# The routed experts of a two-block transformer on one Trainium2 core: all first products before all second products, with the first results in DRAM between them

## What is computed

```python
def one_block(xblk):
    q = (xblk @ w_query).reshape(B, TOKEN_BLOCK, N_PEER_HEADS, 2, SUBKEY_DIM)
    s = jnp.einsum('bthpd,hpnd->bthpn', q, sub_keys).astype(jnp.float32)
    vals, idx = lax.top_k(s, PEER_TOPK)
    cand = (vals[..., 0, :, None] + vals[..., 1, None, :]).reshape(...)
    cand_idx = (idx[..., 0, :, None] * N_KEYS + idx[..., 1, None, :]).reshape(...)
    top_s, pos = lax.top_k(cand, PEER_TOPK)
    eidx = jnp.take_along_axis(cand_idx, pos, axis=-1)
    g = jax.nn.softmax(top_s, axis=-1).astype(xblk.dtype)
    h = jnp.einsum('btd,bthkd->bthk', xblk, expert_u[eidx])
    act = jax.nn.gelu(h, approximate=False) * g
    return jnp.einsum('bthk,bthkd->btd', act, expert_v[eidx])
```

## Time and profile before

| | us |
|---|---|
| median of 3 runs (4229.99 to 4234.79) | 4233.03 |
| the profiled execution | 4228.66 |
| its span in the trace | 4226.9 |
| TensorE busy | 3918.0 (93%) |
| VectorE, ScalarE, GpSimd busy | 2746.0, 1996.5, 96.7 |
| layer 0, from the end of the sub-key scores to the last expert product | 421.1 to 1430.1 |
| layer 1, the same | 1765.2 to 2771.9 |

### The profile page before, as it was taken

One profiled execution on the slowest core, in us unless ns is written; L12 is line 12 of the kernel. 1 busy time (PEld: TensorE's weight loads), 2 busy tenths in 40 slices (PEclk: granted clock), 3 DMA queues, 4 the chain that ended last, 5 costly groups with the idle time before them and its releaser, 6 DMA issues.

```text
span 4226.9 us, 77624 instructions
## 1 busy us (share of the span) xinstructions
PE 3918.0 (93%) x25828; PEld 3362.6 (80%) x25828; DVE 2746.0 (65%) x5370; ACT 1996.5 (47%) x3973; POOL 96.7 (2%) x96
## 2 busy tenths in 40 slices
PE   6989499999999999859999999989999989898998
PEld 2989146999999888714799999979998779898897
DVE  1563976776667665597676677756666665666665
ACT  1554065445544554327554445444454444444444
POOL 0000000000000000000000000001001010101010
PEclk6999599999999999869999999999999999999999
DMA  8435644555555434654455555565554225454453
GB/s 285 153 112 170 243 145 146 186 188 185 188 187 186 163 115 150 209 184 164 153 186 186 188 185 187 186 193 184 167 186 137 93 66 186 140 186 139 140 179 134
DMA packets 195903, 714.34 MB, mean 169 GB/s; under 512 B 21696, under 2 KB 22080, under 8 KB 195520
## 3 DMA queue, kind: packets, MB, share of 16 engines
q1 hardware_dynamic: 194112, 705.08, 50.0%
q0 software_dynamic: 1664, 7.57, 0.7%
HBM read 711.52 MB, written 1.05 MB: 169 GB/s over the span
## 4 chain that ended last, share of the span: by engine, by line
PE 84%; DVE 10%; ACT 2%; DMA 2%; issue 1%; PEldq 0%; SPq 0%; DVEq 0%; ACTq 0%; PEld 0%; POOL 0%
PE bank L1620 16%; PE bank L1622 16%; PE bank L1621 16%; PE bank L1675 8%; PE bank L1676 8%; PE bank L1677 8%; PE bank L1793 4%; PE bank L1955 2%; PE bank L1738 2%; DMA raw<-stream 2%; PE bank L1956 1%; DVE wl L954 1%; PE bank L1926 1%; PE bank L2080 1%; DVE arena L1318 0%
## 5 line engine op out<-in xcount | busy, mean ns | idle before, releaser
L954 DVE TENSOR_TENSOR wl<-raw,wh 128x512 fp32r<-128x512 f32 x2180 | 1508.0, 704 | 1032.0 <-ACT wh L529 999.1
L529 ACT ACTIVATE wh<-raw 128x512 fp32r<-128x512 f32 x2180 | 1345.6, 630 | 1214.0 <-PE bank L1622 758.4
L1620 PE MATMUL bank<-XH,wh 128*128 128x256 f32 x5184 | 1499.3, 289 | 94.3 <-DVE XL L1056 46.1
L1621 PE MATMUL bank<-XL,wh 128*128 128x256 f32 x5184 | 1483.5, 286 | 0.0
L1622 PE MATMUL bank<-XH,wl 128*128 128x256 f32 x5184 | 1483.0, 286 | 0.0
L1620 PEld LDWEIGHTS bank<-XH,wh 128*128 128x128 f32 x5184 | 1008.9, 195 | 129.3 <-issue 79.1
L1621 PEld LDWEIGHTS bank<-XL,wh 128*128 128x128 f32 x5184 | 1012.0, 195 | 14.0 <-issue 1.0
L1622 PEld LDWEIGHTS bank<-XH,wl 128*128 128x128 f32 x5184 | 1010.9, 195 | 0.0
L1675 PE MATMUL bank<-wh,AH 128*128 128x512 f32 x1464 | 574.4, 392 | 0.0
L1676 PE MATMUL bank<-wl,AH 128*128 128x512 f32 x1464 | 573.9, 392 | 0.0
L1677 PE MATMUL bank<-wh,AL 128*128 128x512 f32 x1464 | 569.6, 389 | 0.0
(11 more groups left out here) (237 smaller groups left out, 3458.5 us busy)
## 6 DMA issues: line engine op xcount, KB each, us to landing
raw<-stream SPq DMA_DIRECT2D x1340, 512.0 KB, 3.3
arena<-rpb POOLq DMA_DIRECT2D x4, 1024.0 KB, 20.5
arena<-tables POOLq DMA_DIRECT2D x2, 832.0 KB, 7.4
X<-x_t SPq DMA_DIRECT2D x1, 1024.0 KB, 7.6
arena<-ctx_t POOLq DMA_DIRECT2D x1, 1024.0 KB, 6.4
out_t<-X SPq DMA_DIRECT2D x4, 256.0 KB, 2.1
arena<-tables POOLq DMA_DIRECT2D x1, 608.0 KB, 8.8
cols<-columns SPq DMA_DIRECT2D x1, 218.0 KB, 2.5
```

Of the source, the lines that this page charges most:

```text
L529: act.activation(wh[:, n % 4, :], raw[:, q % 4, HALF * half:HALF * (half + 1)], ACT.Copy).then_inc(hi_ready, 1)
L954: tt_op(wl[:, n % 4, :], raw[:, q % 4, HALF * half:HALF * (half + 1)], wh[:, n % 4, :].bitcast(F32), SUB).then_inc(lo_ready, 1)
L1620: pe.matmul(out, wh[:, n % 4, a:b], moving_h, start=start, stop=False, skip_group_check=check)
L1621: pe.matmul(out, wh[:, n % 4, a:b], moving_l, start=False, stop=False, skip_group_check=check)
```

## The change

**Stream.** `experts.l` becomes `expert_u.l` (128 units) and `expert_v.l` (128 units), each in order. The conditioning stages (`MIXED_ADA`: `ada1.1`, `ada2.0` in layer 0, `ada2.1`, `ada2.2` in layer 1; 96 units per layer) are laid between the first 120 units of `expert_u` in the ring: nine places hold five first-product units and four conditioning units.

**Phase one,** 128 steps u, written out without a loop. TensorE: the first product of tile u, a conditioning unit (four steps of five), at times two transposes, from u = 61 a batch of gates. VectorE: the routing instructions with `feed()`, the low half of the next tile, between them; then per step a `lo` and two one-hots. ScalarE: the high halves of tile u + 1, from u = 60 the weighted one-hots, gelu of tile u into `HS` (two buffers), from u = 62 the copy of a bank into the gates. The gates' product is now of plain fp32 one-hots: four matmuls a batch. All one-hots live in a new area `side`, no longer in `wh`, `wl`. GpSimd issues the store of each gelu result (128 KB) to `h_spill` in DRAM; gelu of u + 2 waits for it.

**Phase two.** SyncE loads the stored results back (four buffers `HV`, in `side`) and the units of `expert_v`, alternately. VectorE multiplies a result by its gates (`gated`, one tile ahead), ScalarE makes the high part `AH` (before: VectorE), VectorE the low part `AL`; TensorE runs the second products alone, back to back.

```diff
-        add(f"ada2_gates.{l}", KT * ADA2_GATES, False)
-        add(f"experts.{l}", 2 * KEYS, True, KEYS)
+        for name in MIXED_ADA[l]:
+            add(name, 48, False)
+        add(f"expert_u.{l}", KEYS, True, KEYS)
+        add(f"expert_v.{l}", KEYS, True)
...
+        u = out[f"expert_u.{l}"]
+        for k in range(MIXED_U):
+            ring[base + 9 * (k // 5) + 2 * (k % 5)] = (u, k)
+        for k in range(MIXED_U, KEYS):
+            ring[base + MIXED_A + k] = (u, k)
+        for a in range(MIXED_A):
+            st = out[MIXED_ADA[l][a // 48]]
+            ring[base + 9 * (a // 4) + 2 * (a % 4) + 1] = (st, a % 48)
...
+        def load_values(l):
+
+            st = stages[f"expert_v.{l}"]
+            sp.wait_ge(onehots_free, 2 + BATCHES * (l + 1))
+            for j in range(8):
+                if j >= 4:
+                    sp.wait_ge(gate_done, KEYS * l + j - 3)
+                sp.wait_ge(h_stored[j % 2], 16 * (KEYS // 2 * l + j // 2 + 1))
+                load_h(l, j)
+                load(st.q + j)
+            for n in range(2):
+                sp.wait_ge(h_stored[n], 16 * KEYS // 2 * (l + 1))
...
-            pick_vectors(f"ada2_gates.{l}", 2)
+            U = stages[f"expert_u.{l}"]
+            for u in range(KEYS):
+                pool.wait_ge(group_free, 2 + U.g + u + 1)
+                pool.dma_start(h_spill[u, :, :], HS[:, u % 2, :]).then_inc(h_stored[u % 2], 16)
...
+                group_done(U, u)
+                if l or u >= 2:
+                    act.wait_ge(h_stored[u % 2], 16 * (KEYS // 2 * l + u // 2))
+                act.activation(HS[:, u % 2, :], banks[4 + (U.g + u) % 2][:, 0:T], ACT.Gelu).then_inc(group_free, 1)
...
+            for b in range(BATCHES):
+                feed()
+                if b or l:
+                    dve.wait_ge(weighted_ready, first + b)
+                tt_op(batch(unweighted), keys, over_tokens(0, b), ALU.is_equal).then_inc(unweighted_ready, 1)
+                dve.wait_ge(onehots_free, first + b + 1)
+                tt_op(batch(hot_j[:, b % 2, :]), keys, over_tokens(1, b), ALU.is_equal).then_inc(onehots_ready, 1)
...
+            with dve.Fori(0, KEYS // 4 - 1) as i:
+                for j in range(2, 6):
+                    lo(V, j, i, 4)
+                    row_lows(j, i)
+                    gated(j + 1, i, 4 * i)
...
+            for u in range(KEYS):
+                pe.wait_ge(group_free, U.g + u + 1)
+                tile(U, u, 0, 0, banks[4 + (U.g + u) % 2][:, 0:T], first_pair)
+                if u == 0:
+                    pe.wait_ge(route_evacuated, 8 * (l + 1))
+                for a in after(u):
+                    ada_unit(first_block + a // KT, a % KT, place[MIXED_ADA[l][a // 48], a % 48])
+                n = block_after(u, 3)
+                if n is not None:
+                    turn_block(first_block + n)
...
+                b = u - GATES_FROM - 1
+                if 0 <= b < BATCHES:
+                    spread_choices(b)
```

More of the change, by code:

```diff
@@ L113, in plan @@
     add("ffn.1.1", 3 * FF_TILES, True, FF_TILES)
-    out, q, s, r, g = {}, 0, 0, 0, 0
+    out, ring, q, s, r, g = {}, {}, 0, 0, 0, 0
     for name, units, split, source, groups in rows:
         out[name] = Stage(name, units, split, source, q, s, r, g)
+        if name.startswith("expert_u"):
+            l = int(name[-1])
+            mix(l, out[MIXED_ADA[l][0]].q)
+        elif not any(name in names for names in MIXED_ADA):
+            for k in range(units):
+                ring[q + k] = (out[name], k)
         q += units
@@ L121, in plan @@
         g += groups
-    return out, placed
+    return out, ring, placed
 COLUMNS = [("c", KT), ("c_2", KT), ("c_ctx", KT), ("final_norm", KT)]
@@ L190, in __call__, with build @@
         return self.at[name]
-def build(nc, ctx, stream, columns, tables, x_in, ctx_in, rpb, out):
-    stages, _ = plan()
+def build(nc, ctx, stream, columns, tables, x_in, ctx_in, rpb, h_spill, out):
+    stages, ring, _ = plan()
+    place = {(st.name, k): q for q, (st, k) in ring.items()}
     made = operands_made()
@@ L408, in _, with released, load @@
         seen = Seen()
-        def released(unit):
-            for st in stages.values():
-                if st.q <= unit < st.q + st.units:
-                    k = unit - st.q
-                    return (lo_ready, 2 * (st.s + k) + 2) if st.split else (raw_used, st.r + k + 1)
+        def released(q):
+            st, k = ring[q]
+            return (lo_ready, 2 * (st.s + k) + 2) if st.split else (raw_used, st.r + k + 1)
+        def load(q):
+            st, k = ring[q]
+            if q >= 4:
+                sp.wait_ge(*released(q - 4))
+            sp.dma_start(raw[:, q % 4, :], stream[st.source + k, :, :]).then_inc(raw_ready[q % 4], 16)
         sp.dma_start(cols[:, :], columns).then_inc(prepared, 16)
@@ L1783, in rows_times @@
-        def rows_times(st, nv, kt, halves=(0, 1), i=0, first=False, last=False):
-            q = st.q + kt
-            n_rows = nv * st.units // KT
-            if kt == 0 and halves[0] == 0:
-                pe.wait_ge(picked, 2 * (blocks[0] + 1) + 2 * i)
-            if halves[0] == 0:
-                pe.wait_ge(raw_ready[q % 4], 16 * (q // 4 + 1) + 32 * i)
-            for half in halves:
-                matmul = pe.matmul(banks[6 + half][0:n_rows, :], pick[:, kt, nv:nv + n_rows],
-                                   raw[:, q % 4, HALF * half:HALF * (half + 1)],
-                                   start=first and kt == 0, stop=last and kt == KT - 1)
-            if halves[-1] == 1:
-                matmul.then_inc(raw_used, 1)
@@ L1819, in _, with ada_unit @@
-        pe.wait_ge(silu_ready, 1)
-        ada("ada1.0")
-        pe.wait_ge(mod_copied, ada_stages[0])
+        def ada_unit(n, kt, q):
+            if kt == 0 and n >= 2:
+                pe.wait_ge(block_copied, n - 1)
+            pe.wait_ge(raw_ready[q % 4], 16 * (q // 4 + 1))
+            for g in range(GROUPS):
+                matmul = pe.matmul(banks[6 + n % 2][GROUP * g:GROUP * (g + 1), 0:BLOCK], vectors[:, kt, :],
+                                   raw[:, q % 4, BLOCK * g:BLOCK * (g + 1)], start=kt == 0, stop=kt == KT - 1,
+                                   tile_position=(0, GROUP * g))
+            matmul.then_inc(raw_used, 1)
@@ L1822, in _ @@
+        pe.wait_ge(silu_ready, 1)
+        for k in range(48):
+            ada_unit(k // KT, k % KT, stages["ada1.0"].q + k)
+            if k > KT and k % KT == 1:
+                turn_block(k // KT - 1)
+        turn_block(5)
+        pe.wait_ge(block_placed, 6)
         for l in range(DEPTH):
@@ L1971, in _, with spread_choices @@
-            turn(st, 2)
-            pe.wait_ge(mod_copied, ada_stages[0])
-            pairs(stages[f"experts.{l}"], 1)
+            U, V = stages[f"expert_u.{l}"], stages[f"expert_v.{l}"]
+            first, first_block = l * BATCHES, 6 + BLOCKS_PER_LAYER * l
+            def spread_choices(b):
+                pe.wait_ge(gate_banks_free, first + b + 1)
+                pe.wait_ge(onehots_ready, first + b + 1)
+                pe.wait_ge(weighted_ready, first + b + 1)
+                for n in range(BATCH):
+                    at = slice(n * P, (n + 1) * P)
+                    last = pe.matmul(banks[b % 2][:, at], by_weight[:, b % 2, at], hot_j[:, b % 2, at], start=True,
+                                     stop=True)
+                last.then_inc(onehots_free, 1)
```

491 lines of the change are left out of this document (227 added, 264 removed).

## The result

| | before | after |
|---|---|---|
| median us (lowest to highest, 4 runs each, same chip) | 4231.51 (4229.99 to 4234.79) | 3926.78 (3925.54 to 3928.62) |
| ratio, 95% interval | | 0.9279 (0.9263 to 0.9295) |
| profiled execution, its span | 4228.66, 4226.9 | 3927.0, 3925.1 |
| layer 0, sub-key scores to last second product | 1009.0 | 855.0 (423.3 to 1278.3) |
| layer 1, the same | 1006.6 | 857.4 (1611.8 to 2469.1) |

The forecast was 3944 us, in a range of 3885 to 4035. The two layers gave 2015.6 - 1712.4 = 303.2 us, and the profiled executions differ by 301.7: the gain lies in the expert layers and nowhere else.

A forecast was written before the change was run, and what follows sets the result against it. Routing was taken as bound by VectorE, gates and experts by TensorE. Per layer, TensorE's 837.4 us plus 20, 3, 2 and 1 gave 863.4, saving 288.8 over both layers: 3944 us, range 3885 to 4035.

The forecast's parts named there:

- turned blocks, choices: Phase one, TensorE: 12 turned blocks and the turned choices take about 6 us per layer.
- second products, change of phase, start: Phase two, per layer: 352.0 us of second products, 2 for the change of phase, 1 for the start.
- The ada unit: Phase one, TensorE: a conditioning unit between tiles costs 0.5 us against 0.43 in a row; 96 units, 48 us per layer.
- list of what would prove it wrong: Wrong if ScalarE waits on stores at gelu, phase two exceeds 2.8 us, or an ada unit between tiles exceeds 0.6.
- The waits in tiles 0 to 60: First 60 tiles: 18 us per five against TensorE's 16.35, so 20 us a layer, plus 3 for table loads.
- The batches: Tiles 61 to 124: a gates batch takes TensorE 1.0 us, 0.1 of it to change over; 64 us per layer.
- Second products: Phase two: TensorE takes 2.75 us per tile, 352.0 per layer, and hides all other engines' work.
- The store path: First results stored to DRAM in phase one: 5.5 us in all, fits two buffers, cost 0.
- slower by the stores: Rival, phase one: a 9.6 us store path would cancel the gain; at 12 us, 4540 us in all; chance 0.05.
- VectorE as the bound of phase two: Rival, second products: VectorE waits for ScalarE's high rows, 3.1 us a tile, 4034 us in all; chance 0.06.
- The ring: Rival, first 60 tiles: four load places set the pace, 20.7 us per five; 4009 us, 4030 with batches; chance 0.10.

## Why the prediction was right, point by point

The time was right to 17 us of 3927 (0.4%), the forecast was the case that came, and the mechanism is shown: the routing and the gates run beside first products, and taking either out brings its time back. But three terms of the sum were mis-sized, by +24, -18 and -7 us a layer, and cancelled each other. That is in part luck: only the first two hang together.

| per layer, us | predicted | measured |
|---|---|---|
| 128 first products | 367.4 | 368.6 (2.88 each) |
| 96 ada units | 48 (0.5 each) | 72 (0.75 each) |
| 64 batches | 64 (1.0 each) | 57 (0.89 each) |
| turned blocks, choices | 6 | 3 (0.2 each, choices 0.65) |
| waits in tiles 0 to 60 | 20 and 3 | 4 to 6 |
| second products, change of phase, start | 352, 2, 1 | 349 |
| sum | 863.4 | 855.0 and 857.4 |

(The measured rows add up to 1 to 2 us less than the layers.)

- **The ada unit** failed as a step: "between tiles of another shape I take 0.5". 0.43 in a row was right, and the 0.07 added for the change of shape should have been 0.32. It was on the prediction's own list of what would prove it wrong (over 0.6), and it cost 24 us a layer. What makes it so is not the shape of the matmul but the division of the array: four column groups of 32 between whole-array matmuls, as the run with the unit on the whole array showed.
- **The waits in tiles 0 to 60** failed in the other direction: 18 us per five tiles against TensorE's 16.35. TensorE's five tiles were really 3.54 + 3 x 3.63 + 2.97 = 17.4 us (3.54 for the tile that has no unit before it), so that they covered VectorE's 16.5 and the DMA engines' 16.6 by 0.8, where the prediction had them 0.2 short, and the waits almost vanished. The two errors hang together: a filler that takes longer hides more. Without the units these tiles stopped at 204 to 208 us, 16.7 to 17.0 per five, where I had put the two at 16.5 and 16.6.
- **The batches** were 0.89, just the eight records of the earlier trace rows without the 0.1 for a change: a whole-array fp32 matmul behind a whole-array fp32r matmul costs no change.
- **Second products** at 2.75 were 2.73 with no first products between them; the 0.02 may be the change of kind at the borders, which the earlier trace rows has in each.
- **The store path** was 4.2 us (0.3 handing over, 3.9 landing, in all 256 between 2.0 and 6.1) against 5.5; two places cover it, and ScalarE waits at most 5 us in all for stores. The rival "slower by the stores", from a path of 9.6 us, was far off: even with one place the kernel stays 5.1% ahead of the one before. The Trainium skill's rule that GpSimd's descriptor writing stalls while VectorE runs an instruction in a two-port mode (SBUF — State Buffer, the "DVE blocks DMA" trap) shows nothing here: the issue took 539 to 570 ns in 256 stores, with VectorE busy for 0.83 of that time in tiles 2 to 59, against the 0.54 of the earlier trace rows. Nearly all of VectorE's work there is on two tensors or the search for the top 16; plain copies, which the rule is about, are few and of 0.2 to 0.6 us, so the rule was hardly put to the test.
- **VectorE as the bound of phase two** was not near: its order has the gate of a tile ready one tile ahead, as the prediction said, and even 0.29 us more a tile cost nothing.
- **The ring** as pace setter did not come by itself, but stands close: pairs of units seem to bring it (8 to 13 us a layer, after what they save), and 12% more bytes bring the DMA engines.

The 4 to 6 us of waits in tiles 0 to 60 have two parts in the trace. In each layer TensorE waits five times for VectorE's low halves, 1.9 and 2.1 us in all, four of them at the same tiles (17, 35, 44, 55) in both layers, which speaks for VectorE's order of steps. Three times it waits for ScalarE's gelu, 1.7 and 3.6 us. The longest, in layer 1, on ScalarE and then TensorE:

```profile
1626.55 1.15 ACT L565 ACTIVATE wh<-raw 128x512 fp32r<-128x512 f32 x2 [4.04 <-DMA raw<-stream]
1627.61 0.36 ACT L819 ACTIVATE side<-bank 128x256 f32<-128x256 f32 x1
1628.05 0.36 PE L1705 MATMUL bank<-XH,wh 128*128 128x256 f32 x1 [1.76 <-ACT side L819]
```

Gelu stands behind the high halves of the next tile, and those waited for a load that landed 7.1 us after its issue, the slowest of these tiles, where the median is 4.6. What stays open is why single loads are so late; taking the stores' bytes away left the waits about as they were (1.1 and 3.6 us in layer 0), and more than four places were not tried.

## What to carry to other kernels

Price a filler between two instructions of another kind from a place where it stands between them, not in a row of its own; where it divides the array in column groups and its neighbours don't, add the change (0.32 us here) once for each time that it is entered, and put fillers in groups where the ring of loads has slack. When one engine's term in a sum grows, take the waits that it covers down again: the terms aren't independent. A result that goes out to DRAM and back in bulk cost nothing here while the places before it covered one landing and the DMA engines had room (0.88 busy; with each store doubled, 0.92, it cost 13.5 us a layer), and how many places are needed is (gelu + hand-over + landing) over the time of a tile: 4.6 / 3.6 gives two.

## What the runs showed of the hardware

- Changing TensorE from the whole array to 32-column groups and back costs 0.32 us at full clock; four matmuls in four such groups take the time of one.
- An fp32 matmul of 128 columns costs 0.22 us and may stand between fp32r matmuls at no further price; two fp32r ones (0.11 apart, 599.96 to 601.00 for eight with a change) cost the same, so it made no difference to TensorE whether a one-hot product was split in two parts.
- After 102 us of standstill TensorE ran its first 24 matmuls 0.21 us apart instead of 0.12, at a granted clock of 0.54, and the next tile was at full clock again: the half clock behind a long wait cost 2.3 us here (5.97 against 3.63), little beside the wait.
- With the DMA engines 0.89 to 0.95 busy, the rate beside compute differed by stretch: 323 GB/s at 0.92, 315 at 0.92 with every store doubled, 314 at 0.89 without ada matmuls, but 333 at 0.91 in layer 1 of that same run and 336 at 0.95 at the start of the kernel before:

```profile
1659.00:1759.00 100.00, 93.05 (x747) 90.05 (x747) 88.14 (x265) 50.97 (x103) 16.73 (x31) 1.00 0.91 333
```

```profile
10.00:85.00 75.00, 52.31 (x394) 11.06 (x394) 0.00 (x0) 2.19 (x9) 0.00 (x0) 0.68 0.95 336
```

The Trainium skill (DMA: Bandwidth & Descriptors, Specifications) gives one core about 358. These stretches of 75 us and more stayed 6% and more below it, so the 323 of the row was the safer figure for the sum, but it isn't a ceiling.
